# Gate and up products of the feed-forwards: the two parts of x side by side in one matmul of 512 columns

## What is computed

```python
def swiglu(h, w13, w2):
    gate, up = jnp.split(h @ w13, 2, axis=-1)
    return (jax.nn.silu(gate) * up) @ w2
```

## Time and profile before

| | us |
|---|---|
| median of three runs | 3854.67 |
| lowest, highest | 3852.77, 3856.65 |
| span of the profiled execution | 3849.5 |
| TensorE busy in the span | 3393.3 |
| VectorE, ScalarE, GpSimd busy | 1697.2, 1594.9, 1221.3 |

### The profile page before, as it was taken

The page is one execution under the profiler, slowest core; times in us unless marked ns, Lnnn a source line. Parts: engine busy times, 40 slices in busy tenths (PEclk is TensorE's granted clock), DMA queues, the critical chain, the costliest instruction groups (busy, mean ns, idle before and its releaser), DMA issues.

```text
span 3849.5 us, 51802 instructions
## 1 busy us (share of the span) xinstructions
PE 3393.3 (88%) x20194; PEld 3007.8 (78%) x20194; DVE 1697.2 (44%) x1948; ACT 1594.9 (41%) x1859; POOL 1221.3 (32%) x509
## 2 busy tenths in 40 slices
PE   6988896897689889895899889886799999999998
PEld 5987895896379879784799878785677777778777
DVE  4233214313421141423222142403488888888887
ACT  2332341332223225331133135230276667667665
POOL 3863681584038436240288255130000000000000
PEclk8998998998689999996999999997899999999999
DMA  4532452352035334340355333330498889889886
GB/s 161 178 142 108 153 184 89 132 185 101 20 111 185 141 122 153 110 164 11 121 185 178 134 137 129 124 131 28 164 350 321 317 320 366 317 317 369 317 317 260
DMA packets 97072, 707.22 MB, mean 184 GB/s; under 512 B 10784, under 2 KB 10784, under 8 KB 10944
## 3 DMA queue, kind: packets, MB, share of 16 engines
q1 hardware_dynamic: 96624, 703.37, 49.5%
q0 software_dynamic: 336, 2.23, 0.1%
HBM read 704.51 MB, written 1.05 MB: 183 GB/s over the span
## 4 chain that ended last, share of the span: by engine, by line
PE 71%; DVE 9%; issue 8%; POOL 5%; ACT 4%; DMA 2%; DVEq 0%; POOLq 0%; SPq 0%; ACTq 0%
PE bank L515 17%; PE bank L516 17%; PE bank L517 17%; PE bank L551 7%; POOL half_lo L474 5%; DVE kept L1359 2%; DMA ring<-experts 2%; PE bank L548 2%; DVE rs L1356 2%; DVE kept L1455 1%; PE bank L811 1%; PE bank L663 1%; PE bank L573 1%; PE bank L585 1%; PE bank L643 1%
## 5 line engine op out<-in xcount | busy, mean ns | idle before, releaser
L474 POOL TENSOR_TENSOR half_lo<-ring,half_hi 128x1024 fp32r<-128x1024 f32 x502 | 1219.4, 2439 | 1320.7 <-ACT half_hi L1039 1320.7
L515 PE MATMUL bank<-h_hi,half_hi 128*128 128x256 f32 x3088 | 886.9, 287 | 93.1 <-DVE h_lo L1369 91.6
L516 PE MATMUL bank<-h_lo,half_hi 128*128 128x256 f32 x3088 | 882.2, 286 | 0.0
L517 PE MATMUL bank<-h_hi,half_lo 128*128 128x256 f32 x3088 | 881.7, 286 | 0.0
L1300 ACT ACTIVATE expert_parts<-ring 128x1024 fp32r<-128x1024 f32 x672 | 674.3, 1052 | 315.6 <-DMA ring<-experts 280.6
L1039 ACT ACTIVATE half_hi<-ring 128x1024 fp32r<-128x1024 f32 x502 | 528.1, 1057 | 659.6 <-PE bank L517 643.0
L515 PEld LDWEIGHTS bank<-h_hi,half_hi 128*128 128x128 f32 x3088 | 600.8, 195 | 99.2 <-DVE h_lo L1369 94.4
L516 PEld LDWEIGHTS bank<-h_lo,half_hi 128*128 128x128 f32 x3088 | 600.7, 195 | 0.4
L517 PEld LDWEIGHTS bank<-h_hi,half_lo 128*128 128x128 f32 x3088 | 600.3, 194 | 0.0
L1793 DVE TENSOR_TENSOR expert_parts<-ring,expert_parts 128x1024 fp32r<-128x1024 f32 x448 | 528.0, 1222 | 82.4 <-ACT expert_parts L1300 80.2
L1381 DVE TENSOR_TENSOR hid<-sg,bank 128x512 f32<-128x512 f32 x58 | 39.9, 688 | 779.8 <-PE bank L517 779.8
(11 more groups left out here) (257 smaller groups left out, 4109.3 us busy)
## 6 DMA issues: line engine op xcount, KB each, us to landing
ring<-experts SPq DMA_DIRECT2D x336, 1024.0 KB, 4.8
ring<-stream SPq DMA_DIRECT2D x330, 1024.0 KB, 4.8
kept<-mem POOLq DMA_DIRECT2D x2, 1024.0 KB, 7.4
con<-consts SPq DMA_DIRECT2D x1, 1473.0 KB, 8.5
kept<-mem SPq DMA_DIRECT2D x1, 1024.0 KB, 5.0
kept<-x_in SPq DMA_DIRECT2D x1, 1024.0 KB, 14.5
out<-kept SPq DMA_DIRECT2D x1, 1024.0 KB, 3.9
par<-params SPq DMA_DIRECT2D x1, 317.5 KB, 8.8
```

The lines of the kernel that those rows point to most:

```text
L474: nc.gpsimd.tensor_tensor(half_lo[:, h % HALVES, :], ring[:, u % RING, s * HALF:(s + 1) * HALF], half_hi[:, h % HALVES, :].bitcast(F32), A ...
L515: mm(dst, w_hi, x_hi, start=start, stop=False, skip_group_check=shared)
L516: mm(dst, w_hi, x_lo, start=False, stop=False, skip_group_check=shared)
L517: return mm(dst, w_lo, x_hi, start=False, stop=stop, skip_group_check=shared)
```

## The change

- h_hi and h_lo become one tensor `h_parts`, in which the 256 high and the 256 low values of a k tile lie side by side.
- `gate_up` no longer uses `products`. For the high part of the weight it issues one matmul of 512 columns (both parts of x), and for the low part one of 256 columns (x_hi) which adds into the first 256 columns of the same bank. A bank now holds one half m: w_hi x_hi + w_lo x_hi in its first 256 columns, w_hi x_lo in its last 256. Gate takes banks 0 and 1, up takes 2 and 3, in each chunk.
- VectorE's `summed` adds the two ranges. It copies w_hi x_lo of both banks to `at_t` and adds the other range, 512 values per partition each; gate goes to sg, up to hid. New semaphores `gate_sum`, `up_sum` and `part_read` order this.
- ScalarE's silu waits for gate_sum and works in place on sg. The product is now sg times hid. TensorE waits for the sums of the chunk before, ahead of overwriting the banks.
- The eight banks are one PSUM tensor; the experts' tensors lie in h_parts.

```diff
-        h_hi = sb("h_hi", [PARTS, KT, TOK], F32R)
-        h_lo = sb("h_lo", [PARTS, KT, TOK], F32R)
+        h_parts = sb("h_parts", [PARTS, KT, 2, TOK], F32R)
+        h_hi, h_lo = h_parts[:, :, 0, :], h_parts[:, :, 1, :]
...
-        bank = [ctx.enter_context(nc.psum_tensor(f"bank{i}", [PARTS, 512], F32)) for i in range(8)]
+        banks = ctx.enter_context(nc.psum_tensor("banks", [PARTS, 8, 512], F32))
+        bank = [banks[:, i, :] for i in range(8)]
...
                 def gate_up(i, u, r=0):
                     for s in range(2):
-                        split_columns(bank[2 * (i % 2) + s], u + s, r, u == u0 and s == 0)
+
+                        wait(pe, (gate_sum, up_sum)[s], 2 * r + (h0 + i))
+                        for m in range(2):
+                            w_hi, w_lo = half(u + s, m, r)
+                            b = bank[2 * s + m]
+                            for k in range(KT):
+                                if u == u0 and s == 0 and m == 0 and k == KT // 2:
+
+                                    pe.wait_ge(h_split, 2 * t.now("split"))
+                                cols = slice(k * PARTS, (k + 1) * PARTS)
+                                mm(b[:, :], w_hi[:, cols], h_parts[:, k, :, :].rearrange("p h t -> p (h t)"),
+                                   start=k == 0, stop=False, skip_group_check=True)
+                                last = mm(b[:, 0:TOK], w_lo[:, cols], h_hi[:, k, :], start=False, stop=k == KT - 1,
+                                          skip_group_check=True)
+                            last.then_inc(first_done if m == 0 else unit_done, 1)
...
                     def silu():
-                        if i >= 2:
-
-                            act.wait_ge(hid_ready, 2 * r + (h0 + i - 1))
-                        nc.scalar.activation(sg[:, i % 2, :], bank[2 * (i % 2)][:, :], ACT.Silu).then_inc(sg_ready, 1)
+                        act.wait_ge(gate_sum, 2 * r + (h0 + i + 1))
+                        nc.scalar.activation(sg[:, i % 2, :], sg[:, i % 2, :], ACT.Silu).then_inc(sg_ready, 1)
...
                 def hidden(i, odd):
+
+                    def summed(dst, b, s):
+                        sums = banks[:, b:b + 2, :]
+                        v.tensor_copy(at_t[:, :].rearrange("p (m t) -> p m t", m=2), sums[:, :, TOK:2 * TOK]).then_inc(part_read, 1)
+                        dve.wait_ge(part_read, 2 * i + (2 * h0 + b // 2 + 1))
+                        v.tensor_tensor(dst[:, odd, :].rearrange("p (m t) -> p m t", m=2), sums[:, :, 0:TOK],
+                                        at_t[:, :].rearrange("p (m t) -> p m t", m=2), ALU.add).then_inc(s, 1)
+
+                    dve.wait_ge(unit_done, ffn_unit(u0, i) + 1)
+                    summed(sg, 0, gate_sum)
+                    dve.wait_ge(unit_done, ffn_unit(u0, i) + 2)
+                    dve.wait_ge(gate_sum, i + (h0 + 1))
+                    summed(hid, 2, up_sum)
+                    dve.wait_ge(up_sum, i + (h0 + 1))
                     dve.wait_ge(sg_ready, i + (h0 + 1))
-                    dve.wait_ge(unit_done, ffn_unit(u0, i) + 2)
-                    v.tensor_tensor(hid[:, odd, :], sg[:, odd, :], bank[2 * odd + 1][:, :], ALU.mult).then_inc(hid_step, 1)
+                    v.tensor_tensor(hid[:, odd, :], sg[:, odd, :], hid[:, odd, :], ALU.mult).then_inc(hid_step, 1)
```

More of the change, by code:

```diff
@@ L254, in two_blocks @@
         hid_step = sem("hid_step")
+        gate_sum = sem("gate_sum")
+        up_sum = sem("up_sum")
+        part_read = sem("part_read")
         quad_read = sem("quad_read")
@@ L396, in two_blocks @@
         scat, ye = page(8, 1), page(6, 1, D)
[L398 to L401, removed]
+        h_flat = h_parts[:, :, :, :].rearrange("p k h t -> p (k h t)")
+        xs_hi, xs_lo = (h_flat[:, i * D:(i + 1) * D].rearrange("p (k s) -> p k s", k=KT) for i in range(2))
+        hT_hi, hT_lo = (h_flat[:, (2 + i) * D:(3 + i) * D].rearrange("p (i c) -> p i c", i=2) for i in range(2))
         w_hi = [expert_parts[:, i, 0:UNIT] for i in range(RING)]
```

## The result

| | before | after |
|---|---|---|
| median, us (runs) | 3853.72 (4) | 3885.27 (4) |
| lowest, highest | 3851.61, 3856.65 | 3883.41, 3890.29 |
| span of the profiled execution | 3849.5 | 3885.3 |

The kernel after is slower: 1.008 times the time of before, 95% interval 1.0066 to 1.0094, 31.6 us by the medians and 35.8 us by the two spans. The forecast was 3892 us, its range 3857 to 3915.

What follows compares the result with a forecast made beforehand. TensorE's matmul stream was taken to bound the kernel, with GpSimd a close second. Matmul savings, silu's delay and the port stalls sum to +30 us, the clock adds 7: 3854.7 + 30 + 7 = 3892 us, range 3857 to 3915.

Steps and rivals of the forecast that it cites:

- Term 1: Gate and up matmuls: a 512- plus a 256-column matmul takes 0.353 us instead of 0.360 for three, saving 13 us.
- rival (c): TensorE's issue pays for the third load, so a pair falls below 0.30 us: -12 us, 3842 us, chance 0.06.
- Term 2: Silu waits for VectorE's copy and add; counted from x, the next unit's first matmul, down stalls 0.27 us per chunk.
- The sign of being right: In each chunk, a short TensorE wait on GpSimd's half behind the gate unit, which ends near x+5.7.
- Term 3: VectorE's SBUF operations behind the up unit wait for GpSimd: 2.8 us idle at down(0) and last down of each feed-forward.
- (b): VectorE's cast and product slip in between GpSimd's operations, shrinking the 2.8 us stalls to 0.3: 3859 us, chance 0.14.
- (d): VectorE's copy from PSUM waits for GpSimd, 1 to 1.4 us late in each chunk: +60, 3950 us, chance 0.08.
- costed at nothing: Effects priced at zero: h_parts' stride, TensorE's waits on the sums, silu's source in SBUF, the experts' buffers, SP's reload.
- Term 4: Clock falls after the ten feed-forward stalls: four counted at 1.7 us each, +7 us, bounds 0 and 20.

Runs made afterwards that it cites:

- e6: Kernel after, with the next high half ahead of silu in the feed-forwards alone and the cast to hid_hi on ScalarE: 3835.02 us, ratio 0.9955 to before.
- e8: Kernel after, with the cast to hid_hi on ScalarE and an early load of silu's table, silu still ahead of the high half: 3850.83 us, ratio 1.0003.
- e2: Kernel after, with the cast to hid_hi moved from VectorE to ScalarE, silu keeping its place: 3856.85 us, ratio 1.0013.
- e3: Kernel after, with a one-element silu at the start of each feed-forward to load its table early: 3879.65 us, ratio 1.0071.
- e1: Kernel after, with the next high half ahead of the unit's own work everywhere `step` is used: 3865.92 us, ratio 1.0047.
- e4: Kernel after, with the next high half ahead of the unit's work everywhere and the cast to hid_hi on ScalarE: 3859.86 us, ratio 1.0016.
- e7: Kernel after, with the next high half ahead of silu in the feed-forwards alone, cast left on VectorE: 3848.32 us, ratio 0.9995.
- e5: Kernel before, with silu also waiting for a VectorE copy and add on the gate bank, result unused: 3864.23 us, ratio 1.0032.

## Why the prediction was right, step by step

**Term 1, the pair.** Expected 0.353, measured 0.3534 (e6); 512-column matmuls are 0.23 to 0.24 apart. The saving of 13 us is there: e6 has 10.8 of it in the feed-forwards. The sustained 131 ns of the Trainium skill (TensorE: Matmul & The Clock Gate, Back-to-back issue gap) is not met in this stream, and rival (c) falls with it.

**Term 2, silu's two operations.** Expected silu at x+1.66, GpSimd at x+3.30 and the low half done at x+5.70; measured x+1.65, x+3.31 and, with 2.40 us, x+5.71. The chunk was to be 17.33 and is 17.27: two units at 5.655 and one at 5.76 are 17.07, so the late start costs 0.20 instead of 0.27. Over 53 chunks this is 3 us to the good. The sign of being right, a short wait in each chunk, showed only as the second matmul at 0.22. e8 against e6 shows the term by itself: a chunk of 17.27 against 17.07.

**Term 3, the port.** Expected: copy and add free of GpSimd, product, cast and `hid_lo` each behind one of its operations, and the end at x+8.6. Measured: 0.69, 0.69, then 1.22, 2.52, 2.79, end x+8.24. The cast, for which no row of before spoke, does wait: e2 takes it off VectorE and the chain is short again. That agrees with the rule weighed there from the Trainium skill (SBUF — State Buffer, Who interferes with whom), now for the cast too. Rivals (b) and (d) fall: the operations did not slip in between, and no copy waited. The 2.8 us at the last down is 2.14 (10.7 / 5). The 2.8 that I put at down(0) is 2.16 to 2.38 in four feed-forwards. In the first it is 0.20, since gate(1) had come late already.

**Two things that were missed.** In "costed at nothing" I looked at silu's source and not at the instruction that belongs to it, its table load. The load, 1.28 us behind the new wait, makes a third idle in each feed-forward, at gate(1). In four of them it is 1.41 us on the mean, where the forecast has 0.27; without the load (e3) 0.25 is left, so that the forecast's term holds and 1.2 us are the table's. In the first it is 3.69. There the forecast has VectorE's copy start 0.20 behind the gate unit, and it started at 2.47, behind other work. The total of idle time came out near the forecast (ten idles of 2.8, 28 us, against fifteen with 29.5) by luck: these two, which I did not have, made up for idles that I had put too high.

**Term 4, the clock.** Expected +7, bounds 0 and 20. Added up over the windows of the five feed-forwards, TensorE was granted half its clock (1.2 instead of 2.4 GHz) for 23.9 us before and 45.8 after: 21.9 us at half speed cost 11 us. Before, each feed-forward has such a time only at its start, behind the wait of 13.6 us for x. After, there are seven more stretches of 3.4 us at half clock, and each begins within 1.3 us of the end of one of the fifteen idles. Ten of these are longer than 2 us, and seven of the ten are followed by such a stretch; none of the four of 1.36 to 1.46 us is. So I counted four falls of ten at 1.7 us each, and seven came, each with 3.4 us at half speed, which is the 1.7. They make 11.9 us; the starts are 1.9 us shorter at half speed than before, which gives 1 back. Why three of the ten kept the full clock stays open: 2.14 us was followed by both. Busy time by stretch of the kernel after, right behind three idles of 2.14, 2.38 and 2.14 us, and in the last row the fall at the second of them by itself; the clock is the third number from the end:

```profile
253.60:260.40 6.80, 6.78 (x44) 6.79 (x45) 0.00 (x0) 0.00 (x0) 0.00 (x0) 0.75 0.43 154
446.00:452.80 6.80, 6.80 (x45) 6.80 (x46) 5.64 (x3) 1.06 (x1) 6.31 (x3) 0.77 0.44 154
611.00:617.00 6.00, 5.99 (x48) 5.82 (x48) 0.00 (x0) 0.00 (x0) 0.00 (x0) 1.00 0.49 175
445.70:449.10 3.40, 3.11 (x14) 3.14 (x15) 3.33 (x3) 0.00 (x0) 3.40 (x3) 0.50 0.03 5
```

**Sum.** 29.5 of idle and 11 of clock, less a remainder of about 1 for the steady state, make the 39.4 us of the feed-forwards. The forecast had 37 for the whole kernel; the spans differ by 35.8, since the rest of it was 3.6 shorter, and the medians by 31.6. The medians differ by less than the spans because of the executions that were profiled. That of after took 3887.11 us, 1.8 above its span and 1.8 above its median; with the same 1.8 on its span, that of before took 3851.3, 2.4 below its median.

**Three expectations failed.** e1 and e4 did by one step: I took `step` for the feed-forward's own, and it serves the attention and the projections. e6 and e7, which differ from e4 and e1 in that alone, are 25 and 18 us faster. Of e4's 22 us outside the feed-forwards 11.4 are the waits for the attention's copy and 8.1 are longer busy time, at the lower clock. e6 came out 7 us below its 3842, though its feed-forwards gained what was expected; the excess lies outside them and has no cause that the runs show.

## What to carry to other kernels

A matmul stream that gets faster by 2% gains nothing if the chain that feeds it gets as much longer: count, from the moment a bank is full, everything queued ahead of the operation that TensorE wants next, and put that operation first, but only in the stage where it is wanted (e6 against e4). When an operand moves from PSUM to SBUF on VectorE, look at what GpSimd does at that time, and consider giving the cast to ScalarE. Steady-state margins say nothing of the first and last chunk, a new wait ahead of an activation can bring a hidden table load into the open, and an engine that is given work on the critical path has to be free at that time in every place (the first feed-forward).

## What the runs showed of the hardware

- A cast of 512 elements from SBUF to SBUF on VectorE takes 0.43 us alone and 2.52 beside a GpSimd that works without a pause; the same cast on ScalarE takes 0.63. Copy and add with a PSUM operand keep 0.69 beside the same GpSimd.
- Beside GpSimd at work without a pause, VectorE's cast and `hid_lo` go at the pace of one per GpSimd operation: 2.52 and 2.77 us on the mean against GpSimd's 2.53, which itself was 2.44 before.
- Silu's table load takes 1.28 us. In the kernels with one wait directly ahead of silu it began before that wait was over: in before it had ended 0.5 us ahead of silu, and in e1, e6 and e7 it began 0.3 to 1.6 us before the sum was ready. In those with two (after, e2, e5) it ran behind the sum. No run was made for this alone. The Trainium skill (ScalarE: Activation LUTs, What ACT_TABLE_LOAD costs) gives the same 1283 ns and adds a drain of about as much; here silu follows 0.01 us behind the load (428.08 to 428.09), and no drain is seen.
- A matmul of 256 columns that starts late is followed by the next after 0.22 us instead of 0.12, even where the wait itself is too short to be shown.
- In the kernel after, seven of ten idles of 2.1 to 3.7 us were followed by 3.4 us at half clock (1.2 GHz), and none of four idles of 1.4 us. In e1 and in e7, one of the five idles of 1.74 us was, too.
